# Counting the sample's search keys on one engine while the prompt is scored

## The reference

```
dots  = einsum('bthd,bsd->bths', qi, ki_all) * (D_IDX ** -0.5)       # 8 index heads of 64
score = einsum('bth,bths->bts', wi, relu(dots))
score = where(causal, score, -inf)
vals, sel = lax.top_k(score, topk)                                   # topk = 256
```

## Time and profile before

| | us |
|---|---|
| median of 3 runs | 4743.97 (4735.40 to 4749.68) |
| the profiled execution: its time | 4742.25 |
| the profiled execution: its span | 4740.70 |
| DVE busy over the span | 2860.3 (60%) |
| ACT busy over the span | 2017.4 (43%) |
| PE busy over the span | 4010.8 (85%) |
| the first count of the search starts at | 1269.15 |
| the last unit of the stage is through on DVE at | 1599.57 |

### The profile page before, as it was taken

The page is one execution under the profiler, slowest core; times in us unless marked ns, Lnnn a source line. Parts: engine busy times, 40 slices in busy tenths (PEclk is TensorE's granted clock), DMA queues, the critical chain, the costliest instruction groups (busy, mean ns, idle before and its releaser), DMA issues. The chain is left out here.

```text
span 4740.7 us, 53550 instructions
## 1 busy us (share of the span) xinstructions
PE 4010.8 (85%) x19170; PEld 3175.4 (67%) x19170; DVE 2860.3 (60%) x4825; ACT 2017.4 (43%) x3077; POOL 374.9 (8%) x315
## 2 busy tenths in 40 slices
PE   8999987666867468874399977999999999999998
PEld 6888876664455325442388866878878787877884
DVE  5678646994478889888578854434534453454320
ACT  3333224552367479884477742133223312322210
POOL 0000002443210011100110000000000000000000
PEclk9999976888867779995699988999999999999967
DMA  5555553223310044422411023323433342334346
GB/s 165 159 170 151 150 144 86 76 77 90 96 29 29 1 150 152 155 105 68 108 40 41 25 77 105 96 85 93 123 109 94 104 132 85 97 90 132 98 134 183
DMA packets 481959, 486.34 MB, mean 103 GB/s; under 512 B 96152, under 2 KB 396152, under 8 KB 473144
## 3 DMA queue, kind: packets, MB, share of 16 engines
q1 hardware_dynamic: 457336, 364.66, 26.8%
q0 software_dynamic: 23104, 118.50, 7.1%
q10 hardware_dynamic: 1280, 0.02, 0.0%
HBM read 422.20 MB, written 60.90 MB: 102 GB/s over the span
## 5 line engine op out<-in xcount | busy, mean ns | idle before, releaser
L2465 ACT ACTIVATE weight_parts<-weights 128x1024 fp32r<-128x1024 f32 x296 | 313.4, 1060 | 1188.2 <-PE acc L2792 554.7
L2792 PE MATMUL acc<-act_T,weight_parts 128*128 128x512 f32 x3072 | 702.5, 391 | 15.3 <-DVE act_T L2587 15.3
L2816 PE MATMUL acc<-weight_parts,hidden_parts 128*128 128x512 f32 x3072 | 702.2, 391 | 9.3 <-DVE product_rows L2594 9.3
L2580 DVE TENSOR_TENSOR weight_parts<-weights,weight_parts 128x1024 fp32r<-128x1024 f32 x296 | 363.1, 1228 | 569.7 <-ACT weight_parts L2465 569.7
L2792 PEld LDWEIGHTS acc<-act_T,weight_parts 128*128 128x128 f32 x3072 | 579.9, 189 | 137.1 <-issue 9.1
L2816 PEld LDWEIGHTS acc<-weight_parts,hidden_parts 128*128 128x128 f32 x3072 | 579.7, 189 | 131.9 <-issue 6.1
L532 PE MATMUL accumulated<-hT,w_in_parts 128*128 128x512 f32 (+1 forms) x1920 | 430.7, 390 | 5.8 <-DVE w_in_parts L385 5.8
L532 PEld LDWEIGHTS accumulated<-hT,w_in_parts 128*128 128x128 f32 x1920 | 367.5, 215 | 67.2 <-DVE w_in_parts L385 7.8
L2675 DVE TENSOR_SCALAR hidden_T<-acc 128x512 f32<-128x512 f32 (+1 forms) x160 | 95.7, 598 | 441.9 <-PE acc L2792 352.7
L306 ACT ACTIVATE w_in_parts<-w_in_raw 128x1024 fp32r<-128x1024 f32 (+1 forms) x140 | 141.9, 1015 | 460.3 <-PE accumulated L532 264.2
L2160 ACT ACTIVATE junk_act<-score,candidate 128x1920 bf16<-128x1920 f32 (+6 forms) x224 | 292.6, 1315 | 93.4 <-DVEq L2226 72.5
(11 more groups left out here) (347 smaller groups left out, 6664.3 us busy)
## 6 DMA issues: line engine op xcount, KB each, us to landing
weights<-in_w_up SPq DMA_DIRECT2D x160, 512.0 KB
weights<-in_w_down SPq DMA_DIRECT2D x160, 512.0 KB
w_in_raw<-in_w_in SPq DMA_DIRECT2D x100, 512.0 KB, 4.0
weights<-in_w_out SPq DMA_DIRECT2D x40, 512.0 KB
w_in_raw<-in_w_in SPq DMA_DIRECT2D x60, 256.0 KB, 3.6
x_sb<-in_x_prompt POOLq DMA_DIRECT2D x4, 2048.0 KB
q_rows<-scratch_qT SPq DMA_DIRECT2D x64, 128.0 KB
mix_in<-scratch_mix POOLq DMA_DIRECT2D x4, 2048.0 KB, 9.0
```

Source lines behind the costliest of these rows:

```text
L2465: act.activation(w2[:, w, 0, :], raw[:, b[0], :], ACT.Copy).then_inc(hi_rdy, 1)
L2580: dve.tensor_tensor(w2[:, w, 1, :], raw[:, b, :], w2[:, w, 0, :].bitcast(F32), ALU.subtract).then_inc(lo_rdy, 1)
L2792: mm = pe.matmul(acc[:, u % 8, 0:w], w2[:, u % 2, b, k * P:(k + 1) * P], aT[:, a, k, 0:w], start=(k == 0 and (a, b) == (0, 0)), stop=(k == ...
L2816: mm = pe.matmul(acc[0:pt, 2 * t + half, :], hs[:, d % 2, a, t * pt:(t + 1) * pt], w2[:, d % 2, b, half * ST:(half + 1) * ST], start=(d == ...
```

## The change

ACT now counts all 4104 columns in one operation. DVE's `count` is gone, with its buffers and its semaphore; PE's fold is one product instead of two and waits for ACT's count alone; `fold_twice` is neither loaded nor waited for; the constant of the comparison follows the new number of columns.

```diff
-        jd_s, ja_s = sb("junk_dve_s", [P, ND_S], BF16), sb("junk_act_s", [P, NA_S], BF16)
-        fold, fold2 = sb("fold", [P, P]), sb("fold_twice", [P, P])
+        ja_s = sb("junk_act_s", [P, NEWC], BF16)
+        fold = sb("fold", [P, P])
...
-                for dst, n in ((biti, "bits"), (bitn, "bits_negated"), (fold, "fold"), (fold2, "fold_twice")):
+                for dst, n in ((biti, "bits"), (bitn, "bits_negated"), (fold, "fold")):
                     sp.dma_start(dst[:, :], io[n]).then_inc(search_rdy, 16)
...
                 def fold_counts(r):
                     pe.wait_ge(as_cnt, r + 1)
-                    pe.wait_ge(ds_cnt, r + 1)
-                    pe.matmul(pc, fold2[:, :], cd[:, :], start=True, stop=False)
-                    pe.matmul(pc, fold[:, :], ca[:, :], start=False, stop=True).then_inc(folded, 1)
+                    pe.matmul(pc, fold[:, :], ca[:, :], start=True, stop=True).then_inc(folded, 1)
...
-                    act.activation(ja_s[:, :], score_s[:, ND_S:NEWC], ACT.Sign, bias=ncf_s[:, 0:1], accum_out=ca[:, 0:1])\
+                    act.activation(ja_s[:, :], score_s[:, 0:NEWC], ACT.Sign, bias=ncf_s[:, 0:1], accum_out=ca[:, 0:1])\
...
-                def count(r):
-                    dve.wait_ge(ds_cnt, r)
-                    dve.tensor_scalar(jd_s[:, :], score_s[:, 0:ND_S], cf_s[:, 0:1], None, ALU.is_ge, ALU.add,
-                                      accum_out=cd[:, 0:1]).then_inc(ds_cnt, 1)
...
-                    if u in round_of:
-                        count(round_of[u])
...
-LEAST_S = float(2 * TOPK - 1 - 2 * NA_S)
+LEAST_S = float(2 * TOPK - 1 - 2 * NEWC)
```

More of the change, by code:

```diff
@@ L904, in score_prompt_and_search_sample @@
         F_s, flip_s = keep["F_s"], keep["flip_s"]
-        jd_s, ja_s = sb("junk_dve_s", [P, ND_S], BF16), sb("junk_act_s", [P, NA_S], BF16)
-        fold, fold2 = sb("fold", [P, P]), sb("fold_twice", [P, P])
-        cd, ca, sel_s = (sb(n, [P, 1]) for n in ("count_dve_s", "count_act_s", "keeps_s"))
+        ja_s = sb("junk_act_s", [P, NEWC], BF16)
+        fold = sb("fold", [P, P])
+        ca, sel_s = (sb(n, [P, 1]) for n in ("count_act_s", "keeps_s"))
         cand_s, ncand_s, D_s = (sb(n, [P, 1], I32) for n in ("candidate_s", "minus_candidate_s", "kept_bit_s"))
@@ L910, in score_prompt_and_search_sample @@
         biti, bitn = sb("bits", [P, 32], I32), sb("bits_negated", [P, 32], I32)
-        search_rdy, cand_rdy, as_cnt, ds_cnt, folded, chain_s = (sem("i_s_" + n) for n in ("const", "cand", "act", "dve", "folded", "chain"))
+        search_rdy, cand_rdy, as_cnt, folded, chain_s = (sem("i_s_" + n) for n in ("const", "cand", "act", "folded", "chain"))
         ROUNDS, EARLY, FOLD, UPDATE = 32, 3, 5, 3
@@ L963, in fold_counts @@
                     pe.wait_ge(as_cnt, r + 1)
-                    pe.wait_ge(ds_cnt, r + 1)
-                    pe.matmul(pc, fold2[:, :], cd[:, :], start=True, stop=False)
-                    pe.matmul(pc, fold[:, :], ca[:, :], start=False, stop=True).then_inc(folded, 1)
-                pe.wait_ge(search_rdy, 64)
+                    pe.matmul(pc, fold[:, :], ca[:, :], start=True, stop=True).then_inc(folded, 1)
+                pe.wait_ge(search_rdy, 48)
                 for r in range(EARLY):
@@ L1043, in update @@
                     dve.sem_inc(cand_rdy, 1)
-                dve.wait_ge(search_rdy, 64)
+                dve.wait_ge(search_rdy, 48)
                 link(dve.memset(cand_s[:, :], 0))
@@ L1049, in _ @@
                 for r in range(EARLY - 1):
-                    count(r)
                     update(r)
@@ L1055, in _ @@
                 dve.tensor_tensor(kiT[:, :].bitcast(F32R), kiT[:, :], kh[:, :].bitcast(F32), ALU.subtract).then_inc(k_lo, 1)
-                count(EARLY - 1)
                 update(EARLY - 1)
@@ L1685 @@
 NCOL = NR // 2 * P
-NA_S = 3200
 NEWC = NCOL + TS
-ND_S = NEWC - NA_S
-LEAST_S = float(2 * TOPK - 1 - 2 * NA_S)
+LEAST_S = float(2 * TOPK - 1 - 2 * NEWC)
 HQ = HEADS * TS
```

## The result

The kernel after takes 4759.59 us (median of 7 runs, 4751.36 to 4766.79), the one before 4742.83 (7 runs, 4732.94 to 4749.68): a ratio of 1.0039, 95% interval 1.0024 to 1.0053, so slower by 11 to 25 us. Forecast were 4753 us with a range of 4737 to 4770. The time lies in the range, 6.6 us above the forecast, and only a third of the chance stood on slower. The kernel after, run again beside the kernel before (e11), gave 1.0036 (1.0022 to 1.0050).

What follows compares the result with a forecast made beforehand. No engine is full; ACT's count sits in series with everything except DVE's backlog. Terms 0.8 + 21.1 - 9.7 - 3.6 - 0.15 + 2.4 = +10.9 us on 4742.25 give 4753 us, range 4737 to 4770.

Steps and rivals of the forecast that it cites:

- ACT's longer count: ACT's count in each round: 904 more columns cost 0.753 us, +21.1 us over the 28 counts of rounds 3 to 30.
- DVE's relief, -9.7: Rounds 3 to 30: without its count DVE adds earlier where ACT waits for it; 6.9 of 9.7 us in seven rounds.
- ACT's waits for DVE: Rows of ACT's idle time in the stage: 22.2 us before, expected down by about 10, not to nothing.
- rival B: In the stage, nothing comes back from DVE because other work fills its place: +20.6 us, 4763; chance 0.12.
- The fold, -3.6 and -0.8: PE's first fold product goes: -3.6 us in rounds 3 to 30, -0.8 at the start.
- The clock, +2.4: PE's longer pause in each count lowers its clock in the equivalent of one or two rounds: +2.4 us.
- Rival A: PE's longer pause sends its clock to the lower level and relus wait for dots: +24.7 us, 4767; chance 0.2.
- Start, +0.8: Rounds 0 to 2: longer counts, less an earlier start and saved fold products, put the first dots 0.8 us later.
- Last round, -0.15: End of the stage: DVE's last additions start behind ACT's first relu instead of DVE's count, -0.15 us.
- Rival C: In the stage, DVE is the bound and ACT's longer count fits in its waits: about -2 us, 4740; chance 0.18.
- The step from the stage to the median: Whole kernel: +10.9 us on the profiled execution's 4742.25 gives 4753, taken as 9 us over the median 4743.97.
- The prediction's sign of being wrong: Outside the changed stage: the forecast is wrong if other stages move by more than a few us.

Runs made afterwards that it cites:

- e11: Kernel after, run again without any edit: stage 342.1 us, ratio 1.0036.
- e3: Kernel before, with ACT counting all 4104 columns while DVE still counts its 904 and the fold keeps two products: stage 351.7 us, ratio 1.0042.
- e4: Kernel after, with ACT counting only the last 3200 columns and the first 904 counted by nobody: stage 319.7 us, ratio 0.9983.
- e2: Kernel before, with only ACT's fold product; DVE still counts its 904 columns, left out of the sum: stage 328.2 us, ratio 0.9999.
- e10: Kernel before, with PE's eight bias products 20 units apart instead of 2: stage 310.2 us, ratio 0.9971.
- e1: Kernel before, run again without any edit: stage 329.8 us against 330.4 the first time, ratio 1.0002.
- e8: Kernel before, with the border moved the other way, ACT counting 2400 columns and DVE 1704: stage 335.0 us, ratio 1.0007.

## Why the prediction was right, and where its steps were not

The stage came to +12.0 us net where the sum had +10.9. The mechanism, a count in series with the loop less a partial relief, is borne out; that the sum came so near is in part luck, because steps that were off in either direction balanced. The steps, one by one:

- ACT's longer count: the price of a column held, 3.71 us for a count against 3.708. That it is nearly all in series is shown by e3 (21.3 of 24.1 us over the whole stage).
- DVE's relief, -9.7: 8.4 by e4 against e2. The size was right, the place given to it only in part. By the table of rounds, with the mean of the two executions, 11 and 21 got shorter and 24 stayed, but 7 and 16 paid the full 0.75, and 27 grew by 0.6 and 19 by 0.4. Had all seven paid in full they would have grown by 5.3 us; they grew by 1.9. So they gave back 3.3 us, the fold's share in them included, where the prediction had 6.9 for DVE alone (rounds 10, 18 and 30 gave 1.6 of 1.8). The rest of the relief came in rounds for which the prediction had put little or nothing. And the reasoning behind it, that DVE's count covers ACT's growth in such rounds, would have made e3 +15; it was +21.3.
- ACT's waits for DVE were to fall by about 10 us. From 22.2 and 19.1 in the two executions before they went to 19.7 and 23.1 after: no fall. Those for PE fell, from 54.7 and 57.9 to 48.6 and 44.8. e2 and e4 show why: the two reliefs work through each other. The fold alone took 7.8 us from the waits for PE and gave DVE 5.8 more; taking DVE's count away then took 7.9 from that. Who is named in a wait is who came last; take that one away and the next is close behind. By the prediction's own sign (waits for DVE staying at 22) this would have been rival B; the sign was a bad one, since e4 shows a relief of 8.4 us with the waits for DVE hardly lower.
- The fold, -3.6 and -0.8: 2.3 in all.
- The clock, +2.4: not separated. Rival A as a cause of the whole is refuted: ACT's waits for PE got shorter, not 15 us longer, and the second execution of the kernel after had 0.73, the clock of the kernel before, with the same stage within 1 us; e2 had 0.70 with a stage shorter than before. In single rounds A's mechanism is there: round 25 took 7.37 and 8.42 us at 1.00 and 0.80 before, and 9.78 both times at 0.67 and 0.71 after, 0.6 to 1.7 us beyond the price of the count. The rule of the Trainium skill that an idle PE starts each burst cold (TensorE: Matmul & The Clock Gate, section "HAM oscillation — how this bites in real kernels") agrees with the trace in so far as filling the pause raised the clock to 0.76 and went with 5 us less in rounds 6 to 30. It doesn't agree in every round: round 28 stayed at 0.99 in e11 with a count of 3.71 us in it.
- Start, +0.8 behind the DMA issues: +0.35. Last round, -0.15: -0.10 in the first pair of executions, but the kernel before alone gave 11.58 and 10.73, so that no agreement can be read from it.
- Rival B, by which nothing comes back from DVE, had +20.6: it is refuted by e4 against e2 (8.4 us) and by the stage's 12.0. Its full price for ACT's count is what e3 showed.
- Rival C is refuted by e3 and e4. DVE, the busiest engine of the stage, gave back 8.4 of 39.3 us. The rule of the Trainium skill to relieve the engine with the highest occupancy first (Perfetto Trace Analysis, section "Identifying the Most-Contended Engine") would have been a poor guide; e10 took 20 us out of the stage and left the work as it was (DVE 258.1 us, ACT 242.6).
- The step from the stage to the median has a slip: a shift of 10.9 us is 10.9 us against the median too, some 4755, and not the 9 that come from taking 4744 from 4753.
- The whole time moved by 17 to 18 us against 12 of the stage. So the outcome that was given most of the chance, a difference too small to be told from none, was not the one that came: the median moved 0.35%, beyond the 0.3% that the prediction had set. By its interval it may still be 0.24%. The prediction's sign of being wrong, other stages that move by more than a few us, was too sharp: 12.5 us in the first pair of profiles, but also 1.5 and 5.6 us between two executions of one program (e1).

## What to carry to other kernels

In this loop, where three engines hand on through rings of three buffers, the long operation that ACT does between its steps was nearly all in series with the loop (21.3 of 24.1 us), even beside 77 us of ACT's idle time. Price such a moved piece of work at its full time on the engine that gets it, and at far less on the engine that loses it: here DVE's 39.3 us gave back 8.4, a fifth. These are prices of this place; with DVE loaded further (e8) its time cost much more. And look where the idle time stands before shifting work into it: here 30 of 77 us were one chain of copies and products, and moving that apart was worth more than any of the three borders between the engines.

## What the runs showed that was not expected

- ACT's waits for DVE were 19.7 us with DVE busy 226 (23.1 in e11), 22.2 at 259 (19.1 in e1), and 49.3 at 282, in e8: flat, and then steep.
- The same round of the same program took 10.25 us at a granted clock of 0.67 and 8.49 at 1.00 (round 22, first execution and e1), while the stage as a whole repeated within 1 us.
- The prompt's search behind the stage took 481 to 482 us from its first count to its last in nine of the fourteen profiles and 486 to 489 in the other five, the same program among both (before 485.7 and 481.7, after 488.8 and 481.1). What sets it is open.
- A wait can move to another row without getting shorter: with ACT's count in two halves, PE's waits for relus at the dots fell from 84.0 to 32.7 us, and 44.7 us of them stood at the fold instead.
